# The state-space block's first three tiles multiply h ahead of the second norm's factor

## The reference

```python
a = jnp.square(jax.nn.relu(u2 @ w_up[l]))
h = h + rmsnorm(a @ w_down[l], norm_mlp_post[l])        # end of the first block
...
shift, scale, gate = adaln(c, w_ada_mix[i], b_ada_mix[i])
h = rms_norm(x, norm_mix_w[i]) * (1.0 + scale) + shift   # start of the second
...
proj = h @ w_in
conv_in, z, xbc, dt_raw, g_conv, g_ssm = jnp.split(proj, splits, axis=-1)
a_half, b_half = jnp.split(conv_in, 2, axis=-1)
u = a_half * jax.nn.sigmoid(b_half)
...
dt = jax.nn.softplus(dt_raw + dt_bias)
```

## Time and profile before

| | us |
|---|---|
| median of three runs | 1712.12 |
| the three runs | 1712.03, 1712.12, 1714.56 |
| the profiled execution, its own time | 1714.21 |
| its span in the profile | 1712.5 |

### The profile page before, as it was taken

How to read it: one execution, slowest core, us unless ns; L and a number is a source line. 1 busy time by engine, 2 the same in 40 slices (tenths; PEclk the granted TensorE clock), 3 DMA queues, 4 the chain that set the end, 5 groups by cost and what they waited for, 6 DMA issues and landing times.

```text
span 1712.5 us, 21876 instructions
## 1 busy us (share of the span) xinstructions
PE 1690.3 (99%) x7968; PEld 1376.0 (80%) x7968; DVE 858.1 (50%) x1346; ACT 699.5 (41%) x965; POOL 794.7 (46%) x608
## 2 busy tenths in 40 slices
PE   8999999899999999999999999999999999999998
PEld 6777778688888888887878888788888888888887
DVE  6234464553616166798797878863343311111113
ACT  5233364431313133447464554784423322222232
POOL 1433353555545455643434434344445444654454
PEclk9999999999999999999999999999999999999999
DMA  5221222254636342233223232222222222332232
GB/s 185 74 89 69 87 86 99 74 221 172 227 117 214 129 169 98 77 124 121 77 100 122 108 112 76 100 95 85 88 98 99 74 98 98 123 123 98 98 123 99
DMA packets 31963, 193.82 MB, mean 113 GB/s; under 512 B 3584, under 2 KB 5632, under 8 KB 13216
## 3 DMA queue, kind: packets, MB, share of 16 engines
q1 hardware_dynamic: 24800, 158.89, 26.1%
q10 hardware_dynamic: 7104, 34.15, 5.8%
HBM read 190.86 MB, written 2.16 MB: 113 GB/s over the span
## 4 chain that ended last, share of the span: by engine, by line
PE 97%; DVE 2%; DMA 0%; ACT 0%; issue 0%; SPq 0%; DVEq 0%; ACTq 0%
PE gemm_bank L474 23%; PE gemm_bank L481 23%; PE gemm_bank L475 23%; PE gemm_bank L528 6%; PE gemm_bank L512 6%; PE gemm_bank L521 3%; PE gemm_bank L516 3%; PE aux_bank L876 1%; PE aux_bank L619 1%; PE aux_bank L881 1%; PE aux_bank L861 1%; PE aux_bank L645 1%; PE aux_bank L636 1%; PE aux_bank L549 0%; DMA h<-x_t_dram 0%; PE aux_bank L854 0%
## 5 line engine op out<-in xcount | busy, mean ns | idle before, releaser
L436 POOL TENSOR_TENSOR w_lo<-w_raw,w_hi 128x512 fp32r<-128x512 f32 x580 | 768.6, 1357 | 896.2 <-ACT w_hi L1119 896.2
L474 PE MATMUL gemm_bank<-a_hi,w_hi 128*128 128x512 f32 x1216 | 483.7, 398 | 0.0
L475 PE MATMUL gemm_bank<-a_lo,w_hi 128*128 128x512 f32 x1216 | 474.1, 390 | 0.0
L1119 ACT ACTIVATE w_hi<-w_raw 128x2048 fp32r<-128x2048 f32 x146 | 278.4, 1907 | 184.9 <-PE gemm_bank L481 124.4
L481 PE MATMUL gemm_bank<-a_hi,w_lo 128*128 128x512 f32 x1232 | 309.8, 394 | 0.0
L481 PEld LDWEIGHTS gemm_bank<-a_hi,w_lo 128*128 128x128 f32 x1232 | 229.2, 188 | 52.7 <-issue 6.0
L474 PEld LDWEIGHTS gemm_bank<-a_hi,w_hi 128*128 128x128 f32 x1216 | 228.4, 188 | 51.4 <-issue 4.8
L475 PEld LDWEIGHTS gemm_bank<-a_lo,w_hi 128*128 128x128 f32 x1216 | 228.5, 188 | 47.5 <-issue 1.9
L2004 DVE SCALAR_TENSOR_TENSOR aux_bank<-scratch,gcol,aux_bank 128x511 f32<-128x511 f32 (+15 forms) x240 | 165.7, 733 | 14.2 <-ACT aux_bank L1345 11.9
L474 PE MATMUL gemm_bank<-b_hi,w_hi 128*128 128x512 f32 x368 | 143.4, 390 | 0.0
L475 PE MATMUL gemm_bank<-b_lo,w_hi 128*128 128x512 f32 x368 | 143.2, 389 | 0.0
(11 more groups left out here) (369 smaller groups left out, 2106.9 us busy)
## 6 DMA issues: line engine op xcount, KB each, us to landing
w_raw<-weights_dram SPq DMA_DIRECT2D x146, 1024.0 KB, 4.7
arena<-ada_dram ACTq DMA_DIRECT2D x32, 768.0 KB, 4.4
acc<-cum_rows ACTq DMA_DIRECT2D x8, 512.0 KB, 3.7
h<-x_t_dram SPq DMA_DIRECT2D x4, 512.0 KB, 7.7
row_b<-cum_rows ACTq DMA_DIRECT2D x4, 512.0 KB, 4.8
scratch<-cum_rows ACTq DMA_DIRECT2D x4, 512.0 KB, 4.0
out_t_dram<-a_raw SPq DMA_DIRECT2D x7, 256.0 KB, 2.3
w_raw<-weights_dram SPq DMA_DIRECT2D x4, 256.0 KB, 6.8
```

What stands on the lines that cost most here:

```text
L436: ins = pool.tensor_tensor(wlo[s][:, w], raw[s][:, w], whi[s][:, w].bitcast(F32), ALU.subtract)
L474: pe.matmul(gemm_bank[bank][:, :], whi[slot][:, w], hi[:, k, :], start=(n == 0), stop=False)
L475: pe.matmul(gemm_bank[bank][:, :], whi[slot][:, w], lo[:, k, :], start=False, stop=False)
L1119: act.activation(whi[panel % 2][:, :], raw[panel % 2][:, :], ACT.Copy).then_inc(w_hi_ready, 1)
```

## The change

It sets the first three tiles on an operand that does not hold the second norm's factor nor the shift, and rebuilds the join around that.

- **The new h** is made by `residual(3)`, as at the first block's other norm: DVE multiplies and DVE adds, chunk by chunk. The sums of gain y squared and of gain y h, the five small steps, POOL's adds and all fifteen transposes are gone.
- **The operand** of the three tiles is `r_hi` = round(h gain2) by ACT and `r_lo` by DVE (`mix_low`). ACT also squares each chunk of h, POOL sums the squares, and PE adds that sum over the partitions between the products with high and low operand. The second factor comes from it and is spread by PE ahead of the last two chunks of the low products.
- **The shift's part** is the product of `shift_pair` (the shift, high and low part, two columns) with the same weights: 16 products of 32 columns and 16 of 256, then three products of one column that turn it onto the partitions (`mix_out`).
- **Factor and shift when read.** DVE multiplies T_DT's 32 rows and the value and gate tile by the factor row in place. ACT adds the shift's part as bias in `dt_x` and in the Sigmoid, and DVE adds it in the value product.
- **All other tiles** still use `a_hi` and `a_lo`. `a_raw` is now made behind T_DT's multiplication, and T_GRP+2 and T_GRP+3 run as a `tile_pair` that waits for `a_hi` chunk by chunk.
- **Panels.** Panel 57 is rounded in two halves around the last square; panel 58's rounding stands ahead of `dt_x` instead of behind it.

```diff
@@ PE
-            sums_of_parts()
-            sums_of_last()
-            keep_busy(1, 3)
-            spread(3)
-            keep_busy(2, 5)
...
+            token_part(sq_sum, True, False)
...
+            dt_shift_products(whi, 0)
+            pe.wait_ge(ysq_ready, 16)
+            token_part(sq[:, 1, :], False, True).then_inc(sum_done, 1)
+            pe.wait_ge(w_lo_ready, P_DT + 1)
+            dt_shift_products(wlo, 1)
             spread(3)
+            pe.wait_ge(w_hi_ready, P_GRP + 1)
+            mix_shift_products(whi, 0)
...
                 for k in range(KC):
+                    pe.wait_ge(raw_hi_ready, k + 1)
+                    pe.matmul(dt_bank, whi[P_DT % 2][:, block(k, 0)], r_hi[:, k, :], start=(k == 0), stop=False)
+                    pe.matmul(dt_bank, wlo[P_DT % 2][:, block(k, 0)], r_hi[:, k, :], start=False, stop=False)
+                    for j in range(2):
+                        pe.matmul(pair[j], whi[P_GRP % 2][:, block(k, j)], r_hi[:, k, :], start=(k == 0), stop=False)
+                    if k == 2:
+                        pe.wait_ge(w_lo_ready, P_GRP + 1)
+                    if k >= 2:
+                        pair_low_weights(k - 2)
+                pair_low_weights(KC - 2)
+                pair_low_weights(KC - 1)
+                mix_shift_products(wlo, 1).then_inc(mix_done, 1)
+                pe.wait_ge(mix_squares, KC - 1)
+                token_part(sq_sum, True, True).then_inc(sum_done, 1)
+                for k in range(KC):
+                    pe.wait_ge(raw_lo_ready, k + 1)
+                    mm = pe.matmul(dt_bank, whi[P_DT % 2][:, block(k, 0)], r_lo[:, k, :], start=False, stop=(k == KC - 1))
...
+                    if k == 5:
+                        spread(4)
...
-                    g(2), g(3)
+                    pe.wait_ge(mix_cols, 1)
+                    tile_pair([(0, P_GRP + 1, T_GRP + j, 0, 0, wide(j)) for j in (2, 3)], a_hi, a_lo,
+                              (a_hi_ready, 3 * KC + 1), (a_lo_ready, 3 * KC + 1), False)
@@ ACT
+            roots(3, sum_done, 4)
+            for k in range(KC):
+                act.wait_ge(h_ready, KC + k + 1)
+                act.activation(r_hi[:, k, :], h[:, k, :], ACT.Identity, scale=gain2[:, k:k + 1]).then_inc(raw_hi_ready, 1)
...
+                act.activation(sq[:, k % 2, :] if k else sq_sum, h[:, k, :], ACT.Square).then_inc(sq_ready, 1)
...
+            roots(4, sum_done, 5)
+            round_weights(0, P_DT + 2, 0, T_DT + 1, 0)
+            act.wait_ge(first_scaled, 1)
+            act.wait_ge(mix_cols, 2)
+            act.activation(dt_x, gemm_bank[T_DT % 4][0:SSM_HEADS, :], ACT.Identity, bias=dt_shift) \
...
-            act.wait_ge(tile_done, T_DT + 1)
-            act.activation(dt_x, gemm_bank[T_DT % 4][0:SSM_HEADS, :], ACT.Identity,
...
-            round_weights(0, P_DT + 2, 0, T_DT + 1, 0)
...
+                    if first and q == 0:
+                        act.wait_ge(first_scaled, 2)
+                        act.activation(u_buf[:, 0, :], src, ACT.Sigmoid, bias=mix_out[:, 1:2]).then_inc(freed(1), 1)
@@ DVE
+            residual(3, "norm_mlp_post", KC, 16)
...
+            for k in range(5):
+                mix_low(k)
+            inverse(4)
+            for k in range(5, KC):
+                mix_low(k)
...
+            dve.wait_ge(tile_done, T_DT + 1)
+            dt_out = gemm_bank[T_DT % 4][0:SSM_HEADS, :]
+            dve.tensor_tensor(dt_out, dt_out, r_row[0:SSM_HEADS, :], ALU.mult).then_inc(first_scaled, 1)
+            for k in range(KC):
+                dve.scalar_tensor_tensor(a_raw[:, k, :], h[:, k, :], gain2[:, k:k + 1], aux[1][:, :],
                                          ALU.mult, ALU.mult).then_inc(pre_raw, 1)
```

More of the change, by code:

```diff
@@ L356, in gc @@
             return gcol[:, c:c + 1]
-        SQ_LN = 3 * KC - 1
+        SQ_LN = 3 * KC
+        mix_bank = gemm_bank[(T_GRP + 2) % 4]
         HALF = (slice(0, S // 2), slice(S // 2, S))
@@ L1614, in inverse @@
                     dve.wait_ge(rinv_ready, n)
-                dve.reciprocal((rinv2 if n == 4 else rinv)[:, :], root[:, :]).then_inc(rinv_ready, 1)
+                dve.reciprocal(rinv[:, :], root[:, :]).then_inc(rinv_ready, 1)
             def normed_shifted(n, q, base, part):
@@ L2020, in ssm_group, with first_value @@
                 dve.wait_ge(gcol_ready, 5 * i + 1)
-                for q in range(2):
-                    src = done(2 * q + 1)
-                    dve.wait_ge(freed(2 * q + 1), free_value(T_GRP + 2 * q + 1) + 4 * i)
-                    src = done(2 * q)
-                    dve.tensor_tensor(u_buf[:, q, :], u_buf[:, q, :], src, ALU.mult).then_inc(u_ready, 1)
+                def first_value():
+                    gate, value = done(1), done(0)
+                    dve.tensor_tensor(gate, gate, r_row, ALU.mult).then_inc(first_scaled, 1)
+                    dve.tensor_tensor(value, value, r_row, ALU.mult).then_inc(first_scaled, 1)
+                    dve.wait_ge(first_scaled, 3)
+                    dve.wait_ge(freed(1), free_value(T_GRP + 1))
+                    dve.scalar_tensor_tensor(u_buf[:, 0, :], value, mix_out[:, 0:1], u_buf[:, 0, :], ALU.add, ALU.mult) \
+                        .then_inc(u_ready, 1)
+                for q in range(2):
+                    if first and q == 0:
+                        first_value()
+                    else:
+                        src = done(2 * q + 1)
+                        dve.wait_ge(freed(2 * q + 1), free_value(T_GRP + 2 * q + 1) + 4 * i)
+                        src = done(2 * q)
+                        dve.tensor_tensor(u_buf[:, q, :], u_buf[:, q, :], src, ALU.mult).then_inc(u_ready, 1)
                     dve.wait_ge(u_ready, 2 * i + q + 1)
```

232 lines of the change are left out of this document (104 added, 128 removed).

## The result

The changed kernel took **1726.6 us** (median of four runs, 1724.4 to 1727.5), the kernel before 1713.3 (four runs, 1712.0 to 1716.1). The ratio is 1.0068, with a 95% interval from 1.0055 to 1.0081: 9 to 14 us slower, 11.7 by the ratio, where 1722.9 (1719.4 to 1727.0) was predicted. One execution of the later run e11 took 1855 us at a mean granted clock of 0.87 and is left out of its median. The profiled execution had a span of 1725.8 us and an own time of 1727.49.

The account below looks back on a forecast made before the run. PE was 97% of the chain, with 12.15 us winnable at the join. The earlier start is spent; two chains behind T_DT add 10.5 us, a later lag 0.3, taking the median from 1712.1 to 1722.9 us (1719.4 to 1727.0).

Parts of the forecast that it names:

- the high end: Top of the forecast range: first three tiles end at 713.5 (+2.4), two more of clock and stalls; 1727.0 us.
- the late operand: Rival: first product waits for something else, three tiles end up to 4 us later, 1726.6; 0.03 shared with later stalls.
- The first part: Up to the first three tiles' end: first product 4.4 us earlier, high phase 12.5 us, end 711.1, as before.
- yardstick: Start of T_GRP+4's low-weight products on PE, 727.97 us before; its shift, forecast +10.5 us, sets the end's shift.
- Behind T_DT: Work queued after T_DT closes at 710.7: PE waits for the exponential until 720.1, 8.8 us of idle PE.
- PE's way: From T_GRP+2's start, near 720.5, to T_GRP+4's low-weight products: 16.3 us plus 1.6 for the clock, reaching 738.4.
- Two chains that meet: Behind T_DT, ACT's then PE's way (738.4) and DVE's (738.5) meet within 0.2 us; removing one brings next to nothing.
- "faster" rival: At turn_steps PE is not held, hold-up shorter than the early start's 2.7 us saving; 1709.4 us, chance 0.05.
- The weights' low part: In the DVE chain behind T_DT: POOL runs beside the first a_lo, adding 0.8 us.
- The lag of 0.3 us behind the join: At the second transposition DVE, 1.5 us later than PE, costs 0 to 0.5 us, taken as 0.3.
- The rule: At ACT's table loads, the skill's about 1380 ns extra drain per switch gives 1724.3; the sum took 1.3 us per change.
- A slow clock for long: Rival: clock stays at 0.50 for all 48 products of T_GRP+2 and T_GRP+3; +20 us, 1732, chance 0.05.

Follow-up runs that it names:

- e11: Changed kernel with seven of eight squarings of the new h on ACT and POOL's seven additions left out; 1725.6 us, ratio 1.0066.
- e6: Changed kernel with exponential and gate early, T_DT's low products first, running sums between T_GRP+4's halves, 22 transposes in PE's short waits; 1725.5 us, ratio 1.0060.
- e3: Changed kernel with ACT's exponential moved behind the second root and DVE's gate and value multiplications moved ahead of a_lo; 1723.1 us, ratio 1.0062.
- e1: Changed kernel with ACT's exponential and its table load moved from behind the eight a_hi to right behind the second root; 1728.0 us, ratio 1.0082.
- e2: Changed kernel with DVE's gate and value multiplications moved right behind a_raw, ahead of a_lo and softplus; 1725.8 us, ratio 1.0075.
- the five edits: Changed kernel with exponential, gate and value multiplications early, T_DT's low products first, value product before softplus, running sums behind T_GRP+4; 1721.1 us, ratio 1.0034.
- e4: Changed kernel with T_DT's eight low products put ahead of the pair's sixteen; 1722.7 us, ratio 1.0054.
- e8: Changed kernel with gate and value multiplications early, 30 transposes ahead of PE's dt_x wait and 80 ahead of the exponential's; 1726.3 us, ratio 1.0064.

## Why the prediction was right

**Direction and size.** Right: slower, and 1726.6 lies in the range, at its upper end. The forecast was +10.8, the rest grew by 11.4; the medians differ by 13.3, and 1.9 us of the profiled pair's 13.3 lie ahead of the join. That spread was not in the prediction; with another like it on top, the time would have left the range, which it met by 0.4 us. (Two of its sums are off by 0.3: the high end adds up to 1727.3, and the late operand, 4 us over the forecast of 10.8, to 1726.9.)

**The first part.** Taken from the yardstick's own start, the first product came at 689.4 where 690.0 was forecast (691.35 less 1.9). The high phase took 13.3 us and not 12.5; e6, with the clock held, gave 12.5, and so did e3, where the half clock fell ahead of the first products. So the pace was right, and what was missing is a half clock over two chunks. The prediction put the half clock only behind the large wait. T_DT closed 31.1 us after the join's start where 30.2 was forecast, within the bounds. The reason given for the pace, ACT's two passes and DVE's two, was half right: e11 shows that DVE's alone set it.

**Behind T_DT.** The wait for the exponential came as forecast, at the place named and released by the instruction named: the product by `neg_exp_a` began 9.0 us after T_DT's closing, forecast 9.4. PE idled 5.98 us there and, which the sum did not name as a wait, 2.17 us for `dt_x` ahead of it. T_DT to T_GRP+4 took 27.7 us, forecast 27.7 by PE's way (710.7 to 738.4). That two terms are off inside it (the clock 1.8 to 1.9 for 1.6, the eight `a_hi` 5.0 for 5.3) cancels; that the sum is exact is luck.

**Two chains that meet.** Right in substance: e1 and e2 alone give 0.7 and 0.1 us there. Panel 59's low part was ready near 740.4 (735.39 and 5.0 us) and PE came for it at 741.15: they met within 0.8 us, not 0.2, and PE's own way was the later one. The picture was still too small. It had two chains; the runs showed four holds, one behind the other: the exponential, panel 59 behind the gate, the softplus ahead of the running sums, and the value tile's bank. The prediction's "faster" rival, which had PE run through `turn_steps`, would thus not have come out faster: e1 did let it through to T_GRP+2 but for the 2.17 us of `dt_x`.

**The weights' low part.** "POOL now runs beside the first `a_lo`, for which I put half as much, 0.8": this step failed. The changed kernel's POOL, four pieces and then the last of them alone:

```profile
715.57 10.54 POOL L439 TENSOR_TENSOR w_lo<-w_raw,w_hi 128x512 fp32r<-128x512 f32 x4 [11.41 <-ACT w_hi L1149]
...
719.27 6.85 POOL L439 TENSOR_TENSOR w_lo<-w_raw,w_hi 128x512 fp32r<-128x512 f32 x1
```

The term was put on the wrong engine. DVE's eight `a_lo` took 5.37 us, no longer than alone, which is most of why its chain came out 0.9 us shorter than forecast (26.9 us from T_DT's closing for 27.8). POOL's four took 10.5 us instead of 5.0, and it cost nothing only because PE came for it at 728.6. In e1, where PE came earlier, it cost 2.4.

**The lag of 0.3 us behind the join** did not appear: PE has no wait from 735 to 770 us, and rest and join grew alike. It appears once a chain is taken away: in e1 PE waits 1.20 us for DVE at 766.29.

**The rule.** The load at 720.98 took 1.28 us and the Exp began 1.29 behind its start; the same at 731.52 and 732.82. By the Trainium skill (ScalarE: Activation LUTs, What ACT_TABLE_LOAD costs) some 1.38 us more of drain were due at each. The first load leaves no room for it on either side, since the last `a_hi` had ended 0.02 us before it began; ahead of the second it could lie in ACT's wait of 7.71 us. T_DT to T_GRP+4 came out at the sum without it.

**The rivals.** A slow clock for long did not come: the stretch 726 to 728 has a mean of 0.79, and it is at 1.00 from 727 on. The operand was not late.

## What to carry to other kernels

When work that ran beside products is put behind a tile's closing, count everything that each queue has to do from there on, not only what the next wait names: here four holds stood one behind the other, and removing one uncovered the next, the first two nearly at the same time. Taking a factor out of an operand saves the wait for it once, but if later tiles need the operand with the factor, it is made twice, and the second making (here 12.6 us of DVE) falls where the engine had its pause. When orders are repaired one by one, follow the busiest queue far behind the join: the five edits gave the join back and still ended 0.34% slower.

## What the runs showed of the hardware

- **DVE can stop GpSimd.** A piece of the weights' low part takes 1.25 us beside `a_raw` (one input in SBUF, one in PSUM) and 6.85 us where it begins 0.19 us ahead of eight `a_lo` (both inputs in SBUF), ending 1.3 us after DVE had finished them: it made no visible progress beside them. The same piece took 6.81 us in e1, 7.01 in e4 and 6.84 in e11. With 1.28 us of multiplications in PSUM between `a_raw` and `a_lo`, e2's four pieces are through in time:

```profile
713.46 4.97 POOL L439 TENSOR_TENSOR w_lo<-w_raw,w_hi 128x512 fp32r<-128x512 f32 x4 [11.17 <-ACT w_hi L1149]
```

  It does not always come to that. Beside `r_lo` (both inputs in SBUF too) POOL's additions and DVE took turns: 1.56 us for an addition instead of 1.30, 1.54 to 1.78 for an `r_lo` instead of 0.74. What decides between the two was not shown. It goes the other way too: DVE's copy of 32 columns within SBUF took 0.17 us in the changed kernel and 1.29 in e1, where POOL was at work on a panel. The Trainium skill (GPSIMD Engine Reference, Key points) says that GpSimd shares its SBUF interfaces with VectorE and contends with VectorE instructions of two SBUF inputs or in a two-port mode; the rows of `a_lo` and `r_lo` agree and give the size, while for the copy they don't tell its mode.
- **The head of the program varies by 3.3 us** over fourteen profiled executions, one of each kernel with the same head (16.95 to 20.28 us to the same products). The rows of the two heads differ in when the granted clock rises and how long PE waits for the first operands. For this kernel it is as large as many an effect that one looks for, and a distance inside the trace avoids it.
- **A transpose of 128x128 as filler costs 0.11 us** at full clock in a row of its own kind, so 110 of them are 12.4 us; e8 had reckoned with 0.07, for waits of 8.1 us, and overshot them.
